# Block products in three wide projections of a two-block transformer kernel

## The chip, the cores and the metric

The kernel runs on one core of a Trainium2 chip. The metric is the time on the device from the start to the end of one execution, in microseconds. All data are fp32.

## What is computed

A first block (a Mamba-2 mixer with a mixture of experts, then differential attention with a mixture of experts) and a second block of two layers (three kinds of attention with a top-k choice of keys, then a gated MLP with a convolution). 256 tokens, width 1024. Cut to the three matrix products that the change touches, and to what is computed beside them:

```python
def diff_attention(x, cos, sin, w_qkv, ...):
    qkv = x @ w_qkv                      # 256x1024 @ 1024x3072
    q, k = apply_partial_rope(q), apply_partial_rope(k)
    ...                                  # 8 heads, two softmaxes each

# second block, each of two layers
z = rms_norm(h, g) @ w_in                # 256x1024 @ 1024x3016
c_q, c_kv, k_pe, dilated qkv, dsa qkv, q_idx, k_idx, w = split(z)
mla:     q = rms_norm(c_q) @ w_uq; kv = rms_norm(c_kv) @ w_ukv; rope
dilated: rope on q and k of 8 heads
dsa:     I[t, s] = sum_h w[t, h] * relu(q_idx[t, h] . k_idx[s])
         keep the 256 best causal keys of each row; rope
```

## The kernel before

The 256 tokens are two tiles of 128 (`tt` or `i` is 0 or 1). Weights come from memory as chunks of 1024 x 512 (2 MB) through `ring`, six slots that SyncE fills in order; a slot is released when the products that read it are done. All other data lie in one area of SBUF, `arena`. The five engines run their own lists of instructions, written out by hand, and wait for each other on semaphores; nothing reorders them.

**The projections.** `attention1` (`x @ w_qkv`) and `attention_layer(l)` for l = 0 and 1 (`h @ w_in`) each take six chunks. `PIECES` lists twelve pieces, a chunk `q` and a token tile. For each, `pe_project` makes eight matmuls of 128x512 (one for each 128 rows of the weights) into one of four PSUM banks, and ScalarE copies the bank to `qkv` or `zz` (`act_project`), in the second block with the row's 1/rms as the scale. The matmul is L1730, the copy L1739. One fp32 matmul stands as two passes in the trace.

**Beside them.** In attention1 VectorE makes the tables of sines, masks (`dve_dil_masks`, L1959 to L1962) and rotates q and k; TensorE then turns the heads (`pe_jobs`, L1759) once all twelve pieces are done, VectorE copies them (`dve_jobs`, L1769), and the attention units begin with L1831. GpSimd makes only `pool_affine` (L442, L443) there. In `attention_layer` VectorE rotates the index columns, normalises the latents (L2471 to L2480), multiplies the index scores by their weights after a relu (L2488), sums them (L2494), takes the best eight and strikes them out, eight times per tile (L2498, L2499), makes the mask, and rotates the MLA and dilated columns (L1799 to L1804). TensorE puts the turns, the index products (L2338) and the latent products (L2364, L2366) between pieces. GpSimd rotates the 512 DSA columns (L1785 to L1790) when all pieces are done.

**The MLP.** `mlp_layer` already makes its products from seven half-size ones. There VectorE forms the weight sums (L2719, L2723, L2725, 128x1024 each), GpSimd the token sums (L2694 to L2712, 128x256 and less), and the convolution's taps are added by VectorE from PSUM (L2737).

## Time and profile before

| | us |
|---|---|
| three runs | 2150.5, 2155.76, 2161.61 |
| median | 2155.76 |
| profiled execution | 2156.95 |
| its span, first to last instruction | 2154.9 |

The mean granted clock of TensorE over the span is 0.929. TensorE is busy for 86% of the span, VectorE for 36%, ScalarE for 18%, GpSimd for 7%.

The profile is read by stretch. The slices of the page show the DMA queues near 100% in the two mixtures of experts and below in the attention and MLP stages. The projections are then read by windows and by TensorE's timeline, and the cost of a new instruction by the groups that keep shapes apart. In the timeline a row is one or more equal instructions in succession; the bracket behind it is how long the engine had been idle, and what ended that.

### The profile page before, as it was taken

The numbers are of one execution on the slowest core, as the hardware profiler recorded it, in microseconds if no ns is written. First come the engines' busy times: TensorE is split into PE (matmuls) and PEld (weight loads), VectorE is DVE, ScalarE is ACT, GpSimd is POOL, SyncE is SP. The second block draws the span as 40 slices with busy tenths as digits, with TensorE's granted clock in tenths as the row PEclk, the third lists the DMA queues.
The fourth block names the chain that finished last, engine by engine and source line by source line (L and its number), as shares of the span: only waits on it lengthen the run. The fifth ranks groups of instructions, "written<-read, shape, count | busy, mean of one in ns | idle before, by whom it ended". The sixth has DMA issues, their size and how long they took to land.

```text
span 2154.9 us, 31628 instructions
## 1 busy us (share of the span) xinstructions
PE 1861.0 (86%) x12701; PEld 1144.9 (53%) x12701; DVE 776.9 (36%) x2404; ACT 380.7 (18%) x1032; POOL 153.5 (7%) x164
## 2 busy tenths in 40 slices
PE   8999999667666689898677676699999999999998
PEld 7687555333333344455333343345588744558873
DVE  4455343221222232653222222348333423833343
ACT  2122121111111111421110111113222101322110
POOL 0112100000000020000000000000002500000350
PEclk9999999988888999899887887899999999999999
DMA  9333379999999974279999999963154227324420
GB/s 353 119 118 117 120 288 424 423 423 422 425 425 423 413 261 156 76 317 422 426 422 423 425 423 423 391 230 117 53 178 147 113 93 267 117 72 163 156 98 30
DMA packets 116986, 565.23 MB, mean 262 GB/s; under 512 B 12968, under 2 KB 16238, under 8 KB 84078
## 3 DMA queue, kind: packets, MB, share of 16 engines
q1 hardware_dynamic: 116846, 563.21, 65.9%
q8 instruction: 107, 1.75, 0.3%
q14 instruction: 33, 0.27, 0.0%
HBM read 562.14 MB, written 1.05 MB: 261 GB/s over the span
## 4 chain that ended last, share of the span: by engine, by line
PE 62%; DMA 21%; SPq 10%; DVE 3%; ACT 2%; issue 2%; DVEq 0%; ACTq 0%
PE ps L2608 14%; DMA ring<-in_moe_w_down_dram 13%; PE ps L1730 12%; PE ps L2638 6%; SPq L844 6%; PE ps L1296 5%; PE ps L700 5%; DMA arena<-in_moe_w_up_dram 3%; PE ps L1402 3%; SPq L850 3%; PE ps L303 3%; PE ps L1306 3%; PE ps L740 2%; DMA arena<-in_moe_w_down_dram 2%; DMA ring<-in_moe_w_up_dram 2%
## 5 line engine op out<-in xcount | busy, mean ns | idle before, releaser
L2608 PE MATMUL ps<-arena,ring 128*128 128x256 f32 (+1 forms) x1536 | 305.5, 362 | 0.0
L2608 PEld LDWEIGHTS ps<-arena,ring 128*128 128x128 f32 x1536 | 271.9, 190 | 33.9 <-issue 1.0
L700 PE MATMUL ps<-ring,arena 128*32 128x256 f32 x2432 | 237.3, 434 | 50.6 <-issue 33.8
L1730 PE MATMUL ps<-ring,arena 128*128 128x512 f32 (+1 forms) x576 | 251.3, 595 | 3.6 <-DVE arena L428 3.6
L700 PE MATMUL ps<-arena 128*32 128x256 f32 x1536 | 179.3, 445 | 39.7 <-issue 29.8
L740 PE MATMUL ps<-ring,arena 128*32 128x256 f32 x1408 | 116.0, 485 | 80.6 <-DMA ring<-in_moe_w_down_dram 77.0
L1730 PEld LDWEIGHTS ps<-ring,arena 128*128 128x128 f32 x576 | 110.0, 193 | 136.3 <-issue 136.1
L700 PEld LDWEIGHTS ps<-ring,arena 128*32 128x32 f32 x2432 | 121.7, 124 | 109.0 <-issue 63.5
L716 DVE TENSOR_TENSOR arena<-arena,ps 64x256 f32<-64x256 f32 x64 | 27.2, 425 | 344.7 <-ACT arena L710 344.7
L2737 DVE SCALAR_TENSOR_TENSOR arena<-ps,pcol,arena 128x255 f32<-128x255 f32 (+1 forms) x176 | 84.9, 482 | 181.3 <-ACT arena L2676 178.2
L700 PEld LDWEIGHTS ps<-arena 128*32 128x32 f32 x1536 | 88.5, 127 | 99.8 <-issue 65.2
L759 DVE COPY h<-ps 32x256 f32<-32x256 f32 x128 | 54.3, 424 | 222.0 <-PE ps L740 221.1
L740 PEld LDWEIGHTS ps<-ring,arena 128*32 128x32 f32 x1408 | 53.4, 132 | 124.8 <-DMA ring<-in_moe_w_down_dram 83.0
L750 ACT ACTIVATE h<-ps 32x256 f32<-32x256 f32 x128 | 47.7, 373 | 396.7 <-PE ps L740 396.0
L1296 PE MATMUL ps<-arena,ring 128*128 128x256 f32 x512 | 116.4, 386 | 1.5 <-DMA ring<-in_ssm_w_in_dram 1.5
L1296 PEld LDWEIGHTS ps<-arena,ring 128*128 128x128 f32 x512 | 98.2, 194 | 15.3 <-issue 2.1
L740 PE MATMUL ps<-arena 128*32 128x256 f32 x640 | 54.9, 499 | 45.1 <-DMA arena<-in_moe_w_down_dram 42.6
L2676 ACT ACTIVATE arena<-ps,pcol 128x256 f32<-128x256 f32 x88 | 49.6, 563 | 232.9 <-PE ps L2608 232.7
L710 ACT ACTIVATE arena<-ps 64x256 f32<-64x256 f32 x64 | 24.0, 375 | 351.7 <-PE ps L700 351.7
L2707 POOL TENSOR_TENSOR arena<-arena 128x256 f32<-128x256 f32 x44 | 55.3, 1257 | 351.7 <-DVE arena L2737 351.7
L2638 PE MATMUL ps<-ring,arena 128*128 128x512 f32 x176 | 76.2, 592 | 0.0
L1574 DVE SCALAR_TENSOR_TENSOR arena<-ps,pcol,arena 128x255 f32<-128x255 f32 (+2 forms) x96 | 46.2, 481 | 62.0 <-ACT arena L1451 59.7
(339 smaller groups left out, 2210.2 us busy)
## 6 DMA issues: line engine op xcount, KB each, us to landing
ring<-in_moe_w_up_dram SPq DMA_DIRECT2D x44, 2048.0 KB, 36.9
ring<-in_moe_w_down_dram SPq DMA_DIRECT2D x44, 2048.0 KB, 35.4
ring<-in_moe_w_gate_dram SPq DMA_DIRECT2D x32, 2048.0 KB, 35.3
ring<-in_w_up_dram SPq DMA_DIRECT2D x22, 2048.0 KB, 8.0
arena<-in_moe_w_up_dram SPq DMA_DIRECT2D x20, 2048.0 KB, 37.2
arena<-in_moe_w_down_dram SPq DMA_DIRECT2D x20, 2048.0 KB, 36.2
...
```

Of the source, the lines that this page charges most:

```text
L303: return nc.tensor.matmul(ps[:, 4 + 2 * tt + half, :], lhs(4 * i + k, tt), w[:, k, half * 512:(half + 1) * 512], start=start, stop=stop)
L700: mm = nc.tensor.matmul(ps[j * CAP:(j + 1) * CAP, 5, 0:256], xg[:, b, (k % 2 * 4 + k // 2) * CAP:(k % 2 * 4 + k // 2 + 1) * CAP], w[k][:, ...
L740: mm = nc.tensor.matmul(ps[j * CAP:(j + 1) * CAP, 7, 0:256], hT[:, b, k % 2, (k // 2) * CAP:(k // 2 + 1) * CAP], wd[:, k, j * 256:(j + 1) ...
L844: sp.dma_start(dst, src[:, lo:hi, :]).then_inc(signal, 16)
L850: sp.dma_start(third_up if slot == 2 else ring.rows8(first + 3 * slot + 1), src).then_inc(signal, 16)
L1296: mm = nc.tensor.matmul(bank[:, 0:SEQ], w[:, k, k4 * P:(k4 + 1) * P], xT[:, k, :], start=(k == 0), stop=(k == KD - 1))
L1306: mm = nc.tensor.matmul(bank, xT[:, k, tt * P:(tt + 1) * P], w[:, k, :], start=(k == 0), stop=(k == KD - 1))
L1402: mm = nc.tensor.matmul(ps[:, part, :], yT[:, 4 * i + k, tt * P:(tt + 1) * P], w[:, k, half * 512:(half + 1) * 512], start=(i == 0 and k = ...
L1730: mm = nc.tensor.matmul(ps[:, bank + n % 4, 0:n_cols], xT[:, k, tt * P:(tt + 1) * P], w[:, k, :], start=(k == 0), stop=(k == KD - 1))
L2608: mm = nc.tensor.matmul(ps[:, n % 4, lo:hi], w[:, k, k4 * P:(k4 + 1) * P], xT_mlp[:, k, lo:hi], start=(k == 0), stop=(k == KD - 1))
L2638: mm = nc.tensor.matmul(ps[:, bank, :], lhs(i)[:, k, :], rhs(i)[:, k, :], start=(i == 0 and k == 0), stop=(i == 5))
L2737: ins = nc.vector.scalar_tensor_tensor(acc, ps[:, n % 4, 0:SEQ - 2 + j], taps2[j][:, n:n + 1], acc, ALU.mult, ALU.add)
```

## The change

Chunk 0 of each projection stays as it was. For chunks 1 to 5 the product of the 256x1024 tokens and the 1024x512 weights is split two by two: tokens into a(row, col), weights into b(row, col) of 512 x 256. Seven products of 128x512 by 512x256 (`BLOCKS`) take the place of eight. Each is four matmuls of 128x256 into one of banks 4 to 7 (`pe_block`, matmul L1804), and waits until the product four before it has been read.

- **Token sums.** VectorE forms S0 to S3 (128x512 each) once per projection.
- **Weight sums.** GpSimd forms T1 to T4 (128x1024 each, both inputs in SBUF) in each of the five chunks (`pool_weight_sum`, L1878, L1883, L1885, L1889). T1 of a chunk waits for P5 of the chunk before, T2 for its P6, T4 for P2 of its own chunk. P5, P6, P7 and P4 of a chunk read T1, T2, T3 and T4.
- **Results.** ScalarE copies P1 to two or three of the four output blocks (`act_first_block`); VectorE adds the other six into them from PSUM (`dve_block`, L1832 in attention1, L1833 with the row's 1/rms): 7 adds per chunk in attention1, 8 in the second block.
- **Ring.** The slots of chunks 1 to 5 are released at P4, the last product.
- **Moved or reshaped.** ScalarE takes the copies of the turned heads. In attention1 the turns are made after chunk 4 and inside chunk 5; `pool_affine` follows the 20 sums. In the second block ScalarE applies the relu to the index scores, and VectorE multiplies and sums them in eight instructions (`index_sums`, L2737 of the kernel after); the choice of the best keys is cut in parts that stand between the adds; the MLA and dilated rotation goes to GpSimd, after the sums of chunks 4 and 5.

```diff
+        BLOCKED = range(1, 6)
+        BLOCKS, BY_DVE = ("P1", "P2", "P6", "P7", "P5", "P3", "P4"), ("P2", "P6", "P7", "P5", "P3", "P4")
+        SUMS = ("T1", "T2", "T3", "T4")
...
+            n = product_count(name, c) - 1
+            if n >= 4:
+                freed, before = BLOCKS[(n - 4) % 7], (n - 4) // 7 + 1
+                if freed == "P1":
+                    pe.wait_ge(block_act.sem, block_act.at(before))
+                else:
+                    pe.wait_ge(block_dve.sem, block_dve.at(read_count(freed, before)))
...
+            elif name == "P6":
+                lhs, rhs = pj.S[1], pj.T2
+                pe.wait_ge(token_summed.sem, token_summed.at(2))
+                pe.wait_ge(weight_summed.sem, weight_summed.at(sum_count("T2", c)))
...
+            for k in range(4):
+                mm = nc.tensor.matmul(ps[:, bank_of(name, c), 0:256], lhs[:, k, :], rhs[:, k, :], start=(k == 0),
+                                      stop=(k == 3))
+            mm.then_inc(block_products.sem, 1)
...
+                (row, col), src = to, ps[:, bank_of(name, c), 0:256]
+                if pj.row_scale is None:
+                    return nc.vector.tensor_tensor(pj.out(c, *to), pj.out(c, *old), src, ALU.add)
+                return nc.vector.scalar_tensor_tensor(pj.out(c, *to), src, pj.row_scale[:, row:row + 1],
+                                                      pj.out(c, *old), ALU.mult, ALU.add)
...
+            if name == "T1":
+                ring.arrived(pool, pj.chunks[c])
+                if c >= 2:
+                    pool.wait_ge(block_products.sem, block_products.at(product_count("P5", c - 1)))
+                ins = nc.gpsimd.tensor_tensor(pj.T1, pj.b(c, 0, 1), pj.b(c, 0, 0), ALU.subtract)
+            elif name == "T2":
+                pool.wait_ge(weight_summed.sem, weight_summed.at(sum_count("T1", c)))
+                if c >= 2:
+                    pool.wait_ge(block_products.sem, block_products.at(product_count("P6", c - 1)))
+                ins = nc.gpsimd.tensor_tensor(pj.T2, pj.b(c, 1, 1), pj.T1, ALU.subtract)
+            elif name == "T3":
+                ins = nc.gpsimd.tensor_tensor(pj.b(c, 0, 1), pj.b(c, 1, 1), pj.b(c, 0, 1), ALU.subtract)
+            else:
+                pool.wait_ge(weight_summed.sem, weight_summed.at(sum_count("T2", c)))
+                pool.wait_ge(block_products.sem, block_products.at(product_count("P2", c)))
+                ins = nc.gpsimd.tensor_tensor(pj.b(c, 1, 0), pj.b(c, 1, 0), pj.T2, ALU.subtract)
+            ins.then_inc(weight_summed.sem, 1)
...
-            for q, c in enumerate(chunks):
-                ring.release(c, projected, PIECES.index((q, 1)) + 1)
-
-        def project_done(chunks):
-            projected.advance(2 * len(chunks))
-            projected_copied.advance(2 * len(chunks))
+            ring.release(chunks[0], projected, 2)
+            for c in BLOCKED:
+                ring.release(chunks[c], block_products, product_count("P4", c))
...
-            pe_project(pe, xT_first, c_qkv, 0, 1, 0, xT_ready)
+            pe_project(pe, pj1, 0, xT_ready)
             pe_turn_normed(pe, 1, -1)
-            pe_project(pe, xT_first, c_qkv, 1, 12, 0, xT_ready)
-            pe.wait_ge(projected_copied.sem, projected_copied.at(12))
-            pe.wait_ge(roped.sem, 1)
-            pe_jobs(pe, head_jobs)
+            for c in BLOCKED:
+                for name in BLOCKS:
+                    pe_block(pe, pj1, name, c)
+                    if (name, c) == ("P2", 1):
+                        pe_project(pe, pj1, 1, xT_ready)
+                    elif (name, c) == ("P4", 4):
+                        pe.wait_ge(roped.sem, 1)
+                        pe.wait_ge(projected_copied.sem, projected_copied.at(2))
+                        pe_jobs(pe, head_jobs[0:4])
+                    elif (name, c) == ("P6", 5):
+                        pe_jobs(pe, head_jobs[4:8], 4)
+            block_done(pe, 5)
...
+            for c in BLOCKED:
+                for name in SUMS:
+                    pool_weight_sum(pool, pj1, name, c)
...
+                if tt == 0:
+                    dve_block(dve, pj1, "P2", 4)
...
+                def index_sums(i):
                     kv = (i + 1) * P
-                    dve.wait_ge(idx_scores.sem, idx_scores.at(i + 1))
-                    for a in range(2):
-                        for m in range(4):
-                            ins = nc.vector.tensor_scalar(idx_terms[:, a, m, 0:kv], ps[:, m, a * SEQ:a * SEQ + kv],
-                                                          0.0, w_idx[:, i, 4 * a + m:4 * a + m + 1], ALU.max,
-                                                          ALU.mult)
-                    ins.then_inc(idx_read.sem, 1)
                     dve.wait_ge(idx_read.sem, idx_read.at(i + 1))
-                    wk = work[:, i, 0:kv]
-                    V(nc.vector.tensor_reduce(wk, idx_terms[:, :, :, 0:kv].rearrange("p a m k -> p k a m"),
-                                              XY, ALU.add))
-                    V(nc.vector.tensor_tensor(wk, wk, caus[i], ALU.add))
-                    for _ in range(TOPK // 8):
+                    for n in range(8):
+                        V(nc.vector.scalar_tensor_tensor(work[:, i, 0:kv], idx_terms[:, n // 4, n % 4, 0:kv],
+                                                         w_idx[:, i, n:n + 1], work[:, i, 0:kv] if n else caus[i],
+                                                         ALU.mult, ALU.add))
...
+                dve_block(dve, pj, "P2", 2)
+                dve_block(dve, pj, "P6", 2)
+                dve_block(dve, pj, "P7", 2)
+                index_sums(0)
+                dve_block(dve, pj, "P5", 2)
+                dve_block(dve, pj, "P3", 2)
+                take_best(0, 0, 2)
+                dve_block(dve, pj, "P4", 2)
+                take_best(0, 2, 6)
+                dve_block(dve, pj, "P2", 3)
...
+                dve_block(dve, pj, "P2", 4)
+                mask_others(1)
+                dve.wait_ge(lat_copied.sem, lat_copied.at(1))
+                lat_heads(0)
+                dve_block(dve, pj, "P6", 4)
+                dve_block(dve, pj, "P7", 4)
+                lat_heads(1)
```

In GpSimd's list, first layer of the second block, this stood before: the affine step of the block before, then the rotation of the DSA columns.

```order
47 L442 TENSOR_TENSOR h<-arena 128x8x128
48 L443 TENSOR_TENSOR h<-h,arena 128x8x128
49 L442 TENSOR_TENSOR h<-arena 128x8x128
50 L443 TENSOR_TENSOR h<-h,arena 128x8x128
51 L1785 TENSOR_TENSOR arena<-arena,cst 128x64
52 L1786 TENSOR_TENSOR arena<-arena,cst 128x64
53 L1787 TENSOR_TENSOR arena<-arena,cst 128x64
54 L1788 TENSOR_TENSOR arena<-arena,cst 128x64
```

After the change, from the same place (T1, T2, T3, T4 of chunks 1 and 2; `piece_ready` counts the block products there, `z_tanh_done` the weight sums):

```order
71 L1878 TENSOR_TENSOR arena<-ring 128x1024 [waits slot1_loaded,moe_down]
72 L1883 TENSOR_TENSOR arena<-ring,arena 128x1024 [waits z_tanh_done,h_ready]
73 L1885 TENSOR_TENSOR ring<-ring 128x4x256
74 L1889 TENSOR_TENSOR ring<-ring,arena 128x4x256 [waits piece_ready,z_tanh_done]
75 L1878 TENSOR_TENSOR arena<-ring 128x1024 [waits piece_ready,slot2_loaded]
76 L1883 TENSOR_TENSOR arena<-ring,arena 128x1024 [waits piece_ready,z_tanh_done]
77 L1885 TENSOR_TENSOR ring<-ring 128x4x256
78 L1889 TENSOR_TENSOR ring<-ring,arena 128x4x256 [waits piece_ready,z_tanh_done]
```

Eight of twenty weight sums are shown; the rotation of the DSA columns comes after all of them.

In VectorE's list, first layer of the second block, the sums and the choice for the first token tile stood in one piece (L2488 to L2499), behind the copies of turned data:

```order
1013 L1769 COPY arena<-ps 128x512
1014 L1769 COPY arena<-ps 128x256
1015 L2488 TENSOR_SCALAR arena<-ps,tiny 128x128 x8
1016 L2494 TENSOR_REDUCE arena<-arena 128x128
1017 L2496 TENSOR_TENSOR arena<-arena,cst 128x128
1018 L2498 MAX arena<-arena 128x8
1019 L2499 MATCH_REPLACE arena<-arena 128x128
1020 L2498 MAX arena<-arena 128x8
```

After the change the adds of block products (L1833) stand ahead of the index sums (L2737), and between the parts of the choice (L2744, L2745):

```order
1025 L2731 MEMSET tiny 128x6
1026 L1833 SCALAR_TENSOR_TENSOR arena<-ps,tiny,arena 128x256 x4
1027 L2737 SCALAR_TENSOR_TENSOR arena<-arena,tiny,cst 128x128
1028 L2737 SCALAR_TENSOR_TENSOR arena<-arena,tiny 128x128 x7
1029 L1833 SCALAR_TENSOR_TENSOR arena<-ps,tiny,arena 128x256 x3
1030 L2744 MAX arena<-arena 128x8
1031 L2745 MATCH_REPLACE arena<-arena 128x128
1032 L2744 MAX arena<-arena 128x8
1033 L2745 MATCH_REPLACE arena<-arena 128x128
1034 L1833 SCALAR_TENSOR_TENSOR arena<-ps,tiny,arena 128x256
```

Four adds moved ahead of the sums; P5 and P3 of chunk 2 are read only behind the eight sums.

In TensorE's list, attention1, the turns of heads (L1759) stood behind all pieces:

```order
474 L412 MATMUL ps<-cst,arena 128x128 x8
475 L1730 MATMUL ps<-ring,arena 128x512 x8
476 L412 MATMUL ps<-cst,arena 128x128 x8
477 L1730 MATMUL ps<-ring,arena 128x512 x88
478 L1759 MATMUL ps<-cst,arena 128x128 x32
479 L1831 MATMUL ps<-arena 128x128 x2
```

After the change the last part of it, chunks 4 and 5 with the turns (L1912) in two groups:

```order
491 L1804 MATMUL ps<-arena 128x256 x4
492 L1804 MATMUL ps<-ring,arena 128x256 x4
493 L1804 MATMUL ps<-arena 128x256 x4
494 L1804 MATMUL ps<-ring,arena 128x256 x8
495 L1912 MATMUL ps<-cst,arena 128x128 x16
496 L1804 MATMUL ps<-ring,arena 128x256 x8
497 L1804 MATMUL ps<-arena 128x256 x4
498 L1912 MATMUL ps<-cst,arena 128x128 x16
499 L1804 MATMUL ps<-ring,arena 128x256 x4
500 L1804 MATMUL ps<-arena 128x256 x4
501 L1804 MATMUL ps<-ring,arena 128x256 x8
502 L1993 MATMUL ps<-arena 128x128 x2
```

Sixteen turns moved ahead of chunk 5, sixteen behind its third and fourth product.

## Rows read from the trace of the kernel before

**Rows 1.** Which stretch: three projections; us, busy by engine (count), clock, DMA share, GB/s

```profile
764.00:850.00 86.00, 85.96 (x200) 38.14 (x200) 15.51 (x49) 10.77 (x20) 9.57 (x3) 0.97 0.54 196
...
1400.00:1480.00 80.00, 80.00 (x235) 37.70 (x234) 46.30 (x156) 14.81 (x32) 0.00 (x0) 1.00 0.58 210
1780.00:1860.00 80.00, 80.00 (x244) 38.24 (x243) 45.96 (x170) 11.03 (x23) 0.00 (x0) 1.00 0.60 222
```

**Rows 2.** Groups by form, TensorE: busy us, mean ns of one

```profile
L2608 PE MATMUL ps<-arena,ring 128*128 128x256 f32 x1280 | 276.6, 379 | 0.0
...
L1730 PE MATMUL ps<-ring,arena 128*128 128x512 f32 x512 | 225.3, 598 | 2.0 <-DVE arena L428 2.0
```

**Rows 3.** Timeline of TensorE, attention1: start us, us, what xcount [idle before]

```profile
764.00 9.55 PE L1730 MATMUL ps<-ring,arena 128*128 128x512 f32 x16 [2.02 <-DVE arena L428]
...
774.26 75.70 PE L1730 MATMUL ps<-ring,arena 128*128 128x512 f32 x176
850.65 3.89 PE L1759 MATMUL ps<-cst,arena 128*128 128x128 f32 x32 [0.69 <-ACT arena L1739]
856.28 0.93 PE L1831 MATMUL ps<-arena 64*128 64x128 f32 x8 [1.74 <-DVE arena L1769]
```

**Rows 4.** Timeline of TensorE, second layer of the second block

```profile
1780.56 33.75 PE L1730 MATMUL ps<-ring,arena 128*128 128x512 f32 x80
...
1830.14 1.15 PE L2338 MATMUL ps<-arena 32*128 32x256 f32 x16
...
1866.81 1.36 PE L1831 MATMUL ps<-arena 96*128 96x128 f32 x7
```

**Rows 5.** Groups by form, GpSimd

```profile
L1533 POOL TENSOR_TENSOR arena<-arena 128x512 f32<-128x512 f32 x16 | 16.6, 1040 | 50.4 <-ACT arena L1479 50.4
...
L2694 POOL TENSOR_TENSOR arena<-arena 128x256 f32<-128x256 f32 x10 | 7.2, 724 | 0.8
...
L442 POOL TENSOR_TENSOR h<-arena 128x1024 f32<-128x1024 f32 x2 | 5.7, 2868 | 508.6 <-ACT arena L398 508.6
L1541 POOL TENSOR_TENSOR arena<-arena 128x256 f32<-128x256 f32 x8 | 5.1, 635 | 19.0 <-DVE arena L1636 19.0
...
L1785 POOL TENSOR_TENSOR arena<-arena,cst 128x64 f32<-128x64 f32 x4 | 1.3, 327 | 863.4 <-ACT arena L1739 863.4
```

**Rows 6.** Timeline of both engines, 1708 to 1713 us

```profile
1708.33 1.57 POOL L2707 TENSOR_TENSOR arena<-arena 128x256 f32<-128x256 f32 x1 [1.88 <-DVE arena L2737]
...
1709.23 1.75 DVE L2725 TENSOR_TENSOR ring<-ring 128x1024 f32<-128x1024 f32 x1
...
1709.98 1.31 POOL L2694 TENSOR_TENSOR arena<-arena 128x128 f32<-128x128 f32 x1
```

**Rows 7.** Groups by form, VectorE

```profile
L2737 DVE SCALAR_TENSOR_TENSOR arena<-ps,pcol,arena 128x255 f32<-128x255 f32 x88 | 42.5, 483 | 178.2 <-ACT arena L2676 178.2
...
L2719 DVE TENSOR_TENSOR arena<-ring 128x1024 f32<-128x1024 f32 x10 | 12.1, 1215 | 0.0
...
L1932 DVE SCALAR_TENSOR_TENSOR arena<-arena,tiny 128x256 f32<-128x256 f32 x8 | 3.9, 484 | 0.3
...
L1932 DVE SCALAR_TENSOR_TENSOR arena<-arena,tiny 128x128 f32<-128x128 f32 x8 | 2.8, 351 | 0.3
...
L1799 DVE TENSOR_TENSOR arena<-arena,cst 128x36 f32<-128x36 f32 x4 | 0.8, 198 | 14.0 <-ACT arena L1739 14.0
```

**Rows 8.** Timeline of both engines, 763 to 768 us

```profile
763.05 3.80 POOL L443 TENSOR_TENSOR h<-h,arena 128x1024 f32<-128x1024 f32 x1
...
764.88 1.99 DVE L262 SCALAR_TENSOR_TENSOR tiny<-tiny 128x1 f32<-128x1 f32 x1
...
767.21 0.16 DVE L262 SCALAR_TENSOR_TENSOR tiny<-tiny 128x1 f32<-128x1 f32 x1
```

**Rows 9.** Windows around the start of attention1's projection

```profile
760.00:764.00 4.00, 1.95 (x8) 1.60 (x9) 2.59 (x7) 1.50 (x4) 3.83 (x2) 0.50 1.03 362
...
768.00:772.00 4.00, 4.00 (x9) 1.67 (x8) 1.22 (x2) 1.23 (x1) 2.53 (x1) 0.88 1.03 387
```

More of the change, by code:

```diff
@@ L1117, in experts_dve @@
                 normalise(1)
+                if layer == 1:
+                    dve.wait_ge(rows_loaded.sem, 64)
+                    dve_second_rows(dve, 0)
                 affine(1)
@@ L1772, in dve_jobs, with act_jobs @@
                 ins.then_inc(jobs_copied.sem, 1)
+        def act_jobs(act, jobs, first=0):
+            for m, (blocks, dst, gain) in enumerate(jobs, first):
+                act.wait_ge(jobs_turned.sem, jobs_turned.at(m + 1))
+                src = ps[0:blocks[0].shape[1], m % 4, 0:len(blocks) * P]
+                if len(dst.shape) == 3:
+                    src = src.rearrange("p (a b) -> p a b", a=dst.shape[1])
+                nc.scalar.activation(dst, src, ACT.Copy, scale=1.0 if gain is None else gain)\
+                    .then_inc(jobs_copied.sem, 1)
         def jobs_done(n):
@@ L2469, in dve_attention @@
                 V(nc.vector.tensor_scalar(w_idx, zz[:, :, Z_W:N_IN2], 256 ** -0.5, None, ALU.mult))
+                nc.vector.memset(rms_t, 0.0).then_inc(ready2.sem, 1)
+                for name in BY_DVE[1:]:
+                    dve_block(dve, pj, name, 1)
                 dve.wait_ge(lat_squared.sem, lat_squared.at(1))
@@ new lines, in dve_attention @@
+                mask_others(1)
[4 more added lines that the diff above has]
+                lat_heads(1)
+                dve_block(dve, pj, "P5", 4)
+                dve_block(dve, pj, "P3", 4)
+                nc.vector.memset(rms_t, 0.0).then_inc(ready2.sem, 1)
+                dve_block(dve, pj, "P4", 4)
+                for name in BY_DVE:
+                    dve_block(dve, pj, name, 5)
```

363 lines of the change are left out of this document (263 added, 100 removed).

## Prediction

> **What bounds the kernel now.** I read the windows of the three projections first [rows 1]. TensorE is busy for 85.96 of 86 us in attention1 and for all 80.00 us in each layer of the second block, at a granted clock of 0.97 to 1.00 of full speed. VectorE is busy for 15.5 us there in attention1 and for 46 us in the second block, GpSimd for 9.6 us and nothing. The DMA share is 0.54 to 0.60, so the weights come ahead of use. The projections are bound by TensorE alone: 1 us of matmul removed is 1 us gained, for as long as TensorE never waits. The timelines of TensorE show no idle time between the pieces [rows 3, 4]. The stage behind attention1 streams the experts' weights and starts when the ring's slots come free, so a shift of an attention stage passes on to the end one to one.
>
> **What the change removes.** A pass of 128x512 takes 0.429 us: 80 passes in 33.75 us with the neighbours' overlap give 0.42 to 0.43 [rows 4], 176 in 75.70 give 0.430 [rows 3], and the group gives 225.3/512 = 0.44 with the slow-clock ones in it. A pass of 128x256 takes 276.6/1280 = 0.216 us [rows 2]. A chunk was 16 matmuls of two passes, 32 x 0.429 = 13.7 us; it becomes 28 of two passes, 56 x 0.216 = 12.1 us. The gain is 1.63 us a chunk, 8.15 a projection, 24.4 us in all. In attention1 half of the turns (3.89 us) with the idle 0.69 and 1.74 us around them [rows 3] come inside the projection, where copies lie beside products: another 2.4 us.
>
> **What GpSimd gets.** 20 sums of 128x1024 per projection. No row has this form with both inputs contiguous in SBUF. From 64 to 256 elements a sum goes from 327 to 724 ns, 2.07 ns an element [rows 5]; continued to 1024 that is 0.72 + 768 x 0.00207 = 2.3 us. Lower end: from 256 to 512 elements it goes from 635 to 1040 ns, 1.58 ns an element, which gives 1.85 us. Upper end: L442, 128x1024 with one strided side, 2.87 us [rows 5]. I take 2.3, since it comes from the same kind of sums (L2694) as the new ones. Four sums are 9.2 us of a chunk's 12.1 us. T1 to T3 start together when P5 of the chunk before ends and run for 6.9 us; P6 comes 6.9 us and P7 8.7 us behind that P5, and T2 is ready after 4.6, T3 after 6.9 us. Undisturbed, GpSimd keeps up with 1.8 to 2.3 us to spare.
>
> **What it does to VectorE.** This is the term that decides. In the MLP both engines do weight and token sums side by side [rows 6]: GpSimd's L2707 runs from 1708.33 to 1709.90; VectorE's L2725, begun at 1709.23, ends 1.08 us behind that end; and GpSimd's next, begun at 1709.98, ends only behind L2725. They take 1.57 and 1.75 us, where the same forms alone take 0.72 [rows 5] and 1.22 us [rows 7]. At 764.88 it is plainer [rows 8]: a VectorE instruction on a single column, 0.16 us alone, takes 1.99 us, because L443 of GpSimd, begun at 763.05, ends at 766.85. So a VectorE instruction with two inputs from SBUF stands still until the sum that runs on GpSimd is over, and they take turns, one for one. L2737, with PSUM as one of its inputs, has a mean of 483 ns [rows 7] and shows nothing of the kind beside GpSimd's token sums; the 115 new adds are of its form, 0.48 us each, and I charge them no waits.
>
> The Trainium skill says this in "SBUF — State Buffer", section "Who interferes with whom": a VectorE instruction with two SBUF inputs contends with a GpSimd instruction that reads SBUF, and whoever holds the shared port pair blocks the other fully; with at most one SBUF input and no two-port mode there is no contention. By that rule the trace agrees (1.99 us for 0.16). It speaks against this change, for a burst of T1 to T3 can hold up three VectorE instructions for a sum each. If one took rows 6 to be a slowdown by some tenths only, the sum below would end below the time before.
>
> What has two SBUF inputs on VectorE in the second block: the rotations (six instructions each, 0.2 us and up [rows 7]), the index sums, eight of 0.35 us for tile 0 and eight of 0.48 for tile 1 [rows 7], the masks, the token sums, parts of each 1/rms. In all VectorE has about 56 us of own work in 85 us of projection; adds are 40 x 0.48 = 19 us of it. Each stretch of such work that meets a burst is longer by up to 6.9 us, and the adds queued behind it on VectorE come later. Product n waits until product n-4 was read, so TensorE stops.
>
> **The walk**, with those durations in the order of the new lists; "stall" is TensorE idle.
> - attention1. The lambda and mask instructions (from 789.6 before) stand ahead of P6's add in chunk 1 and meet T1 to T3 of chunk 2: P6 is read at 798.6, P4 waits, stall 7.1 us. The rotation of q and k, 12 large instructions, stands in chunk 4 and meets T3, T4 and the next T1 to T3: stall 7.5 us, in front of the first turns. Stalls 14.6, gains 8.15 + 2.4 and a little cover: +4.4 us.
> - second block, layer 0. 1/rms comes late, stall 2.6; the index rotation in chunk 1 meets T1 to T3 of chunk 2, and `ready2` comes 6.9 us later: stall 9.0. Then as layer 1. In sum +20.8 us.
> - layer 1. The first part is just in time (0.6 us to spare). `index_sums(0)`, 3.1 us of work, meets T1 to T3 of chunk 3 and lasts from 1810.7 to 1819.1: stall 4.4. `index_sums(1)` meets the burst of chunk 4, from 1829.3 to 1838.9: stall 2.5, and 2.4 more at the choice. `mask_others(1)` and `lat_heads(0)` meet that of chunk 5: stall 7.3. 16.6 of stalls and 0.7 of ends, less 8.15: the units start at 1876.0 in place of 1866.81 [rows 4], +9.2 us.
>
> Sum: 4.4 + 20.8 + 9.2 = +34.4 us.
>
> **The clock.** Around attention1's start TensorE was busy for 1.95 of 4 us and the granted clock is 0.50 [rows 9]; the first 16 passes took 9.55 in place of 6.9 us [rows 3]. So a long stop can cost another 2.7 us afterwards. There are five stalls of 7 us or more: 0 to 13 us, I take 3. On the other side the units of attention1 begin with TensorE warmer: 0 to 2 us back. Net +1.
>
> Profiled execution 2156.95 + 34.4 + 1 = 2192; the median of the runs is 1.2 us below the profiled one, so 2190 us. With sums of 1.85 us a burst is 5.6 us and the same walk gives about +28 less 6 where rotations slip between bursts: 2178. Should every other stall be half hidden, 2165. With the clock's upper end 2203.
>
> **What a rule would have instead.** The Trainium skill, "GPSIMD Engine Reference", section 4.1, gives an elementwise sum of two inputs to VectorE, as about twice as fast. On this kernel's rows, VectorE's 128x1024 takes 1.22 us [rows 7] against my 2.3: 20 sums would be 24 us on an engine with 56 of work in 85, and nothing would contend. By that rule the change put the sums on the wrong engine. That is also an experiment.
>
> **Rivals.**
> - *The queues keep up* (other side). The bursts fall between VectorE's two-input stretches, or the adds' slack of four products (6.9 us) absorbs a burst. Then the gain stands: 2156.95 - 24.4 - 2.4 - 2 = 2129, range 2124 to 2145. For it: the slack is as long as a burst, and VectorE is busy for 66% only. Against: two-input work is placed directly in front of adds, in each of the chunks 1 to 5. It decides from the point at which all stalls together stay below 16 us.
> - *The gain is eaten up.* Half of the collisions happen, stalls of 27 us in place of 60: 2157, within 0.5%.
> - *GpSimd becomes the bound.* Sums at L442's 2.87 us: 11.5 of 12.1 us a chunk, T3 is ready 8.6 us behind P5 with 0.05 to spare, and every turn that VectorE takes, and the rotations now in its list (12 and more instructions after chunk 4), delay a product of TensorE directly. 2 to 4 us a chunk over 15 chunks less what is counted above: 2205 to 2215.
>
> **How the numbers follow.** Forecast (stalls exceed the gain, 2165 to 2205) 0.47, GpSimd the bound 0.12, gain eaten up 0.16, queues keep up 0.25. Slower by over 0.5% (10.8 us, about what a measurement can tell from no change) is 0.47 + 0.12 = 0.59; within it 0.16; faster 0.25. Both signs hold much, so the range has to reach from the rival's 2130 to 2210; the likeliest one's own range is 2165 to 2205.
>
> **What would show it.** Right: in the new trace VectorE's L2737 (`index_sums`) has a mean of over 0.8 us in place of 0.35 to 0.48, single ones 2 us and more; TensorE's timeline has idle times of 4 to 9 us behind `<-DVE` at P4 of chunks 1 and 4 and at P2 of chunk 3; L1878 to L1889 take 2.3 us alone; the adds stay at 0.48 us. The units of layer 0 start about 21 us later in their stage, those of layer 1 about 9. Wrong: TensorE's busy share stays at 1.00 from chunk 1 to 5; or its waits name GpSimd, which is the third rival; or sums of under 1.5 us. The walk is weakest in layer 0, where several short works stand close together, and where 5 us either way hang on the order in which two engines reach the same point.

## The result

| | us |
|---|---|
| before, median of four runs beside the change | 2156.07 (2150.5 to 2161.61) |
| after, median of four runs | 2191.85 (2185.03 to 2196.41) |
| ratio after to before | 1.0164, interval 1.0149 to 1.0179 |
| span of the profiled execution after | 2190.4, granted clock 0.921 |

The change makes the kernel slower by 1.6%. The forecast was 2190 us. Below, a stop is a time in which TensorE stands idle.

### The profile page after: what moved, and what is told of

It is laid out like the page before. It is cut to its first block, busy times and chain, and to the rows that moved or that the text cites. A ratio compares the mean times of both kernels' runs of the same rounds, so it can differ in the third digit from the quotient of the medians.

```text
span 2190.4 us, 32731 instructions
## 1 busy us (share of the span) xinstructions
PE 1850.2 (84%) x13061; PEld 1221.1 (56%) x13061; DVE 866.8 (40%) x2435; ACT 399.1 (18%) x1088; POOL 315.7 (14%) x276
## 4 chain that ended last, share of the span: by engine, by line
PE 55%; DMA 20%; SPq 10%; DVE 9%; ACT 2%; issue 2%; DVEq 0%; ACTq 0%
PE ps L2875 14%; DMA ring<-in_moe_w_down_dram 13%; PE ps L2905 6%; SPq L848 6%; PE ps L704 5%; PE ps L1303 5%; PE ps L1804 5%; DMA arena<-in_moe_w_up_dram 3%; PE ps L303 3%; PE ps L744 3%; PE ps L1409 3%; PE ps L1313 3%; SPq L854 2%; DMA arena<-in_moe_w_down_dram 2%; DMA ring<-in_moe_w_up_dram 2%
## 5 line engine op out<-in xcount | busy, mean ns | idle before, releaser
L2875 PEld LDWEIGHTS ps<-arena,ring 128*128 128x128 f32 x1536 | 271.9, 190 | 33.9 <-issue 1.0
L704 PE MATMUL ps<-arena 128*32 128x256 f32 x1536 | 170.3, 431 | 39.4 <-issue 27.5
L1878 POOL TENSOR_TENSOR arena<-ring 128x1024 f32<-128x1024 f32 x15 | 35.7, 2382 | 1150.6 <-DMA ring<-in_w_in_dram 595.8
L1804 PE MATMUL ps<-ring,arena 128*128 128x256 f32 x600 | 149.5, 402 | 40.6 <-DVE arena L1833 26.9
L720 DVE TENSOR_TENSOR arena<-arena,ps 64x256 f32<-64x256 f32 x64 | 27.2, 425 | 352.6 <-ACT arena L714 352.5
L3004 DVE SCALAR_TENSOR_TENSOR arena<-ps,pcol,arena 128x255 f32<-128x255 f32 (+1 forms) x176 | 84.8, 482 | 181.4 <-ACT arena L2943 178.2
L1804 PEld LDWEIGHTS ps<-ring,arena 128*128 128x128 f32 x600 | 118.7, 202 | 63.5 <-DVE arena L1833 30.4
L744 PE MATMUL ps<-arena 128*32 128x256 f32 x640 | 58.0, 523 | 43.8 <-DMA arena<-in_moe_w_down_dram 41.5
```

Source lines behind the costliest of these rows:

```text
L704: mm = nc.tensor.matmul(ps[j * CAP:(j + 1) * CAP, 5, 0:256], xg[:, b, (k % 2 * 4 + k // 2) * CAP:(k % 2 * 4 + k // 2 + 1) * CAP], w[k][:, ...
L744: mm = nc.tensor.matmul(ps[j * CAP:(j + 1) * CAP, 7, 0:256], hT[:, b, k % 2, (k // 2) * CAP:(k // 2 + 1) * CAP], wd[:, k, j * 256:(j + 1) ...
L1804: mm = nc.tensor.matmul(ps[:, bank_of(name, c), 0:256], lhs[:, k, :], rhs[:, k, :], start=(k == 0), stop=(k == 3))
L2875: mm = nc.tensor.matmul(ps[:, n % 4, lo:hi], w[:, k, k4 * P:(k4 + 1) * P], xT_mlp[:, k, lo:hi], start=(k == 0), stop=(k == KD - 1))
L3004: ins = nc.vector.scalar_tensor_tensor(acc, ps[:, n % 4, 0:SEQ - 2 + j], taps2[j][:, n:n + 1], acc, ALU.mult, ALU.add)
```

## The profile after

The same three stretches as [rows 1], moved with the start of each projection (columns: us, busy time of PE, PEld, DVE, ACT, POOL with counts, granted clock, DMA share, GB/s):

```profile
764.00:850.00 86.00, 72.33 (x285) 55.92 (x286) 48.57 (x81) 10.43 (x23) 43.58 (x18) 0.89 0.48 175
1407.30:1487.30 80.00, 70.87 (x302) 53.42 (x300) 67.82 (x156) 19.32 (x47) 40.76 (x28) 0.93 0.50 182
1805.40:1885.40 80.00, 66.36 (x301) 51.80 (x300) 70.92 (x163) 14.65 (x37) 47.37 (x31) 0.94 0.53 196
```

TensorE, busy for all of every stretch before, is busy for 72.33 of 86, 70.87 of 80 and 66.36 of 80 us. VectorE's time rose from 15.5 to 48.6 and from 46 to 68 and 71 us; the new adds are 15 and 19 us of it. GpSimd is busy for half of each stretch, as worked out. The shares of the DMA engines did not rise.

TensorE's timeline of attention1 answers [rows 3]; the second fence, of the second block's layer 1, answers [rows 4]:

```profile
763.87 8.49 PE L1770 MATMUL ps<-ring,arena 128*128 128x512 f32 x16 [2.02 <-DVE arena L428]
...
797.15 7.23 PE L1804 MATMUL ps<-ring,arena 128*128 128x256 f32 x24 [6.69 <-DVE arena L1832]
...
842.47 3.78 PE L1804 MATMUL ps<-ring,arena 128*128 128x256 f32 x8 [6.99 <-DVE arena L1832]
846.04 3.16 PE L1912 MATMUL ps<-cst,arena 128*128 128x128 f32 x16
...
863.55 0.93 PE L1993 MATMUL ps<-arena 64*128 64x128 f32 x8 [0.51 <-DVE arena L1832]
```

```profile
1798.99 6.28 PE L1770 MATMUL ps<-ring,arena 128*128 128x456 f32 x16
...
1845.23 3.68 PE L1804 MATMUL ps<-ring,arena 128*128 128x256 f32 x8 [3.80 <-DVE arena L1833]
...
1865.15 1.99 PE L1804 MATMUL ps<-ring,arena 128*128 128x256 f32 x8 [0.93 <-DVE arena L1833]
...
1874.39 1.99 PE L1804 MATMUL ps<-ring,arena 128*128 128x256 f32 x8 [2.07 <-DVE arena L1833]
1883.03 7.02 PE L1804 MATMUL ps<-ring,arena 128*128 128x256 f32 x24 [6.64 <-DVE arena L1833]
...
1902.23 1.99 PE L1993 MATMUL ps<-arena 96*128 96x128 f32 x12
```

Each stop shown ends with an add of a block product (L1832, L1833) on VectorE. Layer 0 has stops of 2.71, 3.88, 0.92, 2.07 and 6.64 us; the first of them ends with a copy of ScalarE, the others with such adds. All stops of the three projections together are 44.1 us. From the projection's start to the first attention unit it is 99.68 us in attention1 (92.28 before), 111.21 in layer 0 (94.74) and 103.24 in layer 1 (93.25). The starts of the three projections stand 640.96 and 394.16 us apart (633.53 and 376.03 before) and from the last start to the end of the span it is 391.4 us (381.3 before). So attention1 cost 7.4, layer 0 18.1 and layer 1 10.1 us: 35.6 us, the whole difference of the spans (35.5). Of this 33.9 us lie ahead of the first attention units, and 1.7 us behind the first unit of layer 0.

What VectorE did in the first stop, with GpSimd beside it (both engines, start, us):

```profile
788.88 2.51 POOL L1878 TENSOR_TENSOR arena<-ring 128x1024 f32<-128x1024 f32 x1 [9.19 <-PE ps L1804]
789.23 2.58 DVE L2122 SCALAR_TENSOR_TENSOR cst<-cst,arena 128x384 f32<-128x384 f32 x1
791.47 2.53 POOL L1883 TENSOR_TENSOR arena<-ring,arena 128x1024 f32<-128x1024 f32 x1
791.84 2.31 DVE L2123 TENSOR_TENSOR cst<-cst 128x128 f32<-128x128 f32 x1
793.97 2.38 POOL L1885 TENSOR_TENSOR ring<-ring 128x1024 f32<-128x1024 f32 x1
794.19 2.45 DVE L2124 TENSOR_TENSOR cst<-cst 128x256 f32<-128x256 f32 x1
796.67 1.92 DVE L1832 TENSOR_TENSOR arena<-arena,ps 128x256 f32<-128x256 f32 x4
```

Three mask instructions with two inputs in SBUF, which took 0.56, 0.29 and 0.43 us before, take 2.58, 2.31 and 2.45 us, one for each sum T1, T2, T3. P6's add, the first of the four in the last row, is behind them. That is the mechanism of [rows 8], now three times in a row. The groups by form of GpSimd and VectorE say the same in the mean:

```profile
L1883 POOL TENSOR_TENSOR arena<-ring,arena 128x1024 f32<-128x1024 f32 x15 | 36.0, 2400 | 11.8 <-DVE h L632 10.7
L1878 POOL TENSOR_TENSOR arena<-ring 128x1024 f32<-128x1024 f32 x15 | 35.7, 2382 | 1150.6 <-DMA ring<-in_w_in_dram 595.8 <-DMA ring<-in_attn_w_qkv_dram 508.8 <-PE ps L1804 45.9
```

```profile
L1833 DVE SCALAR_TENSOR_TENSOR arena<-ps,tiny,arena 128x256 f32<-128x256 f32 x80 | 36.7, 481 | 34.0 <-PE ps L1804 30.2 <-ACT arena L1818 1.5
...
L2737 DVE SCALAR_TENSOR_TENSOR arena<-arena,tiny 128x256 f32<-128x256 f32 x14 | 18.6, 1328 | 0.5
...
L1832 DVE TENSOR_TENSOR arena<-arena,ps 128x256 f32<-128x256 f32 x35 | 14.7, 420 | 36.6 <-PE ps L1804 35.7
...
L2737 DVE SCALAR_TENSOR_TENSOR arena<-arena,tiny 128x128 f32<-128x128 f32 x14 | 12.9, 924 | 0.5
```

A sum takes 2.38 to 2.49 us (the forecast's 2.3). The index sums take 0.92 and 1.33 us on the mean in place of the 0.35 and 0.48 of the same form in [rows 7]. The adds from PSUM take 0.48 and 0.42 us, where the forecast charged 0.48 for all; those that ran beside a weight sum took the same.

## The experiments

Each was timed beside the kernel before on the same chip, and ratios are to that kernel. It took 2157.43 us beside the first four experiments and 2154.07 us beside the last three, and each ratio is known to about 0.2% (4 us), so small differences between two experiments are read from the traces and not from the times. Code is cut to the lines that matter.

### Without the weight sums

```diff
-                lhs, rhs = pj.S[0], pj.T1
+                lhs, rhs = pj.S[0], pj.b(c, 0, 0)
...
-            for c in BLOCKED:
-                for name in SUMS:
-                    pool_weight_sum(pool, pj1, name, c)
```

> The changed kernel with all 60 weight sums on GpSimd left out (P5 and P6 read blocks of the weights as they are, P7 and P4 read unsummed ones); everything else in place and in order. Theory (each VectorE instruction with two SBUF inputs waits for a whole sum on GpSimd): TensorE's idle times of 3.8 to 7.0 us in the projections vanish, TensorE waits for under 8 us in all three together instead of 43.5, and with the stops the half-speed stretches behind them go; time 2128 us (2120 to 2140), VectorE's index sums (L2737) at 0.35 and 0.48 us. Rival (the adds of block products merely stand behind too much work in VectorE's list, whatever GpSimd does): at least 25 us of waiting stay, time 2160 to 2180.

TensorE's waits for the weight sums go with them. The products are made of unsummed weights, so this run measures time and gives no usable projection.

Measured: 2127.65 us, ratio 0.9854 (0.9837 to 0.9871), as expected. A stretch of 80 us of layer 0, from 5.8 us behind the start of its projection (2.5 in the stretch of the change):

```profile
1390.10:1470.10 80.00, 80.00 (x390) 64.71 (x389) 54.14 (x177) 22.31 (x55) 8.33 (x26) 1.00 0.55 203
```

TensorE is busy for 80.00 of 80 us, and there is no stop over 0.3 us in the three projections but one of 0.51 us ahead of attention1's first unit. Projection to first unit takes 82.4, 87.9 and 84.8 us where before it was 92.3, 94.7 and 93.3. The index sums are back at 0.35 and 0.49 us. The order of VectorE's list is untouched, so the rival that blames the order alone falls. This run takes away TensorE's own waits for GpSimd as well; but no stop of the changed kernel names GpSimd, and the next runs keep those waits. It also measures what the block products are worth when nothing stands in their way: 28.4 us of span, against the 24.4 + 2.4 + up to 2 of the forecast.

### The same sums in four pieces each

```diff
+            def parts(out, x, y):
+                for k in range(0, 4, 1):
+                    ins = nc.gpsimd.tensor_tensor(out[:, k:k + 1], x[:, k:k + 1], y[:, k:k + 1], ALU.subtract)
+                return ins
...
-                ins = nc.gpsimd.tensor_tensor(pj.T1, pj.b(c, 0, 1), pj.b(c, 0, 0), ALU.subtract)
+                ins = parts(pj.T1, pj.b(c, 0, 1), pj.b(c, 0, 0))
```

> Each weight sum on GpSimd is made as four instructions of 128x256 in place of one of 128x1024. Theory (turns are taken instruction by instruction): a two-input instruction of VectorE waits 0.7 us at most in place of 2.4, so stretches of few instructions get shorter (attention1's masks: stall 6.7 to about 2.5; rotation of q and k: 7.0 to about 4), the eight index sums gain nothing (eight turns cost 8 x 0.72), and GpSimd's own work rises from 9.6 to 11.6 of 12.1 us a chunk; time 2180 us (2170 to 2190). Rival (the two engines share a resource in proportion, or GpSimd's total work is what matters): the longer bursts make every stall longer, 2200 us or more.

Measured: 2164.1 us, ratio 1.0035 (1.0018 to 1.0052), below the range expected. GpSimd and VectorE at the index sums of tile 0, layer 1:

```profile
1812.10 2.83 POOL L1876 TENSOR_TENSOR arena<-ring 128x256 f32<-128x256 f32 x4 [2.41 <-PE ps L1804]
...
1814.38 5.17 DVE L2742 SCALAR_TENSOR_TENSOR arena<-arena,tiny 128x128 f32<-128x128 f32 x7
1815.00 2.93 POOL L1876 TENSOR_TENSOR arena<-ring,arena 128x256 f32<-128x256 f32 x4
...
1817.89 2.92 POOL L1876 TENSOR_TENSOR ring<-ring 128x256 f32<-128x256 f32 x4
...
1820.51 1.78 PE L1804 MATMUL ps<-ring,arena 128*128 128x256 f32 x7 [1.41 <-DVE arena L1833]
```

Seven index sums take 5.17 us (6.68 beside whole sums), about one piece of 0.72 us each. Total work on GpSimd grew (11.7 us a chunk, 9.7 with whole sums), yet the kernel is 28 us faster than with whole sums. So what counts is how long one instruction on GpSimd is, and how many of VectorE's meet it. The theory's sign is right and the rival is out. The size was 28 us in place of my 12. The masks' stop fell from 6.69 to 2.47 us as expected; that at the rotation of q and k fell from 6.99 us to nothing (I expected 4), and those behind the first index sums from 3.88 and 3.80 to 0.74 and 1.41 us (I expected no gain). All stops fell from 44.1 to 27.2 us; slow passes behind them, which I had not counted, went with some. In the profiled execution 5.6 us of the difference stand ahead of attention1's projection, where the two kernels are equal; whether the other runs have that too is not known. One stop of the third rival's kind appeared, 1.12 us with GpSimd as the releaser in attention1. And layer 0 stopped for 6.06 us at its first turns, which the next runs explain.

### TensorE kept busy in four of the stops

```diff
                 for name in BLOCKS:
+                    if (name, c) in (("P4", 1), ("P4", 4)):
+                        pe_stay_awake(pe, 2, 7)
                     pe_block(pe, pj1, name, c)
...
+                        if (name, c) == ("P4", 4):
+                            pe.wait_ge(lat_copied.sem, lat_copied.at(1))
+                            pe_stay_awake(pe, 2, 7)
                         pe_block(pe, pj, name, c)
```

> The changed kernel with seven matmuls of 128x512 (6.0 us) that no one reads, put in front of P4 of chunks 1 and 4 in attention1 and of chunk 4 in each layer of the second block, where TensorE stands still for 6.6 to 7.0 us. Theory (a stop costs again in granted clock afterwards): the slow passes behind these four stops go (1.9 + 3.1 + 2.1 + 1.7 us), time 2183 us (2180 to 2187). Rival (the clock falls for another reason, or the stops hide it): 2190 to 2194.

Measured: 2186.93 us, ratio 1.0138 (1.0116 to 1.0159): some 5 us less than the change alone, but the intervals of the two ratios overlap, so the time alone does not decide. The windows of both around the stop in chunk 4 of attention1, first of the change, then of this kernel:

```profile
840.00:844.00 4.00, 1.53 (x4) 1.26 (x5) 3.60 (x7) 0.00 (x0) 1.26 (x1) 0.50 0.00 0
844.00:848.00 4.00, 4.00 (x16) 3.42 (x15) 0.84 (x2) 0.61 (x2) 0.00 (x0) 0.50 0.20 29
```

```profile
840.00:844.00 4.00, 3.00 (x13) 1.92 (x12) 3.53 (x8) 0.00 (x0) 0.77 (x1) 1.00 0.00 0
844.00:848.00 4.00, 4.00 (x28) 3.72 (x27) 0.42 (x1) 2.58 (x6) 0.00 (x0) 1.00 0.66 242
```

After 6.99 us without work TensorE has a granted clock of 0.50 (1.2 GHz) for more than 4 us; kept busy, 1.00 (2.4 GHz). P4's eight passes take 3.78 us in the one and 1.99 in the other. From start to first unit attention1 takes 95.24 in place of 99.68 us, the layers 109.81 for 111.21 and 101.26 for 103.24, 7.8 us in all of the 8.8 expected, although the first passes of attention1 and layer 0 were 1.3 and 0.4 us slower in this execution. Of attention1's 4.4 us only 1.7 are left at the start of the next projection, and the median shows 4.9 in all. That the slow passes come from the stops is shown by the granted clock and the times of the passes (3.78 and 1.99 us); the saving in the total is likely and not more.

### The sums on VectorE

```diff
+        def dve_piece(dve, pj, name, c):
+            dve_block(dve, pj, name, c)
+            if name == "P2":
+                dve_weight_sum(dve, pj, "T4", c)
+            elif name in ("P5", "P3", "P4") and c < 5:
+                dve_weight_sum(dve, pj, {"P5": "T1", "P3": "T2", "P4": "T3"}[name], c + 1)
```

> All weight sums are made by VectorE between its adds (T4 behind P2, T1, T2, T3 of the next chunk behind P5, P3, P4); GpSimd keeps its rotations and the affine step. Theory (the exclusive use of the SBUF port pair is the cost): no VectorE instruction of these stretches takes over 1.3 us; in attention1 VectorE has room (about 55 of 82 us), so the stage gains its 8 to 12 us; in the second block it has about 81 us of work for 77 us of TensorE's, so 5 to 12 us of waiting stay in each layer and the gain is about used up; time 2148 us (2138 to 2165). Rival (VectorE lacks throughput, GpSimd's port does not matter): 24 us more work per projection on the busy engine, time 2200 us or more.

Measured: 2145.08 us, ratio 0.9935 (0.9918 to 0.9952), as expected. It is 47 us less than the change (49 by the ratios), with 24 us more of work per projection on the busier engine: 60 sums of 1.22 us. Attention1 takes 82.74 us (82.39 without any sums), layer 0 95.72 and layer 1 91.81, with stops of 7.1 and 4.8 us left in the layers. The rival (VectorE lacks throughput, 2200 us or more) is out; whether the stops left in the layers are lack of time or order of work is tested by the last run. This is also the experiment that the forecast named where it set VectorE against GpSimd for these sums: here the slower engine was not too slow, it was in the way.

### The affine step first, and an odd mask

```diff
+            pool.wait_ge(rows_loaded.sem, 32)
+            pool_affine(pool)
             for c in BLOCKED:
                 for name in SUMS:
                     pool_weight_sum(pool, pj1, name, c)
-            pool.wait_ge(rows_loaded.sem, 32)
-            pool_affine(pool)
...
-                    V(nc.vector.tensor_scalar(wk, wk, TAKEN, NEG, ALU.not_equal, ALU.mult))
+                    nc.vector.tensor_scalar(wk[:, 0:kv - 1], wk[:, 0:kv - 1], TAKEN, NEG, ALU.not_equal, ALU.mult)
```

> The changed kernel with two small edits in different stages. In attention1 GpSimd's affine step (L442, L443) stands again ahead of the 20 weight sums: the first attention unit waited 4.17 us for VectorE, whose L2092 took 3.00 us beside L443. Theory: that wait falls to about 1.4 us as in the kernel before, and the weight sums of chunk 1, now starting near 775 us, are still ready for P6 at 783: time 2188 us (2185 to 2191). Rival (the wait belongs to the unit itself): no change, 2191 to 2195. In the second block the mask's TENSOR_SCALAR, which took 2.18 us beside a weight sum with only one SBUF input, is made on an odd number of columns (127 or 255, and one more instruction for the last column). If the even count let it into a two-port form, it now takes under 0.6 us, and the next instruction waits in its place, so that no time is won; if any VectorE instruction is stopped by GpSimd, it stays at 2 us.

Measured: 2194.61 us, ratio 1.0193 (1.0169 to 1.0216). No gain: it is above the range expected, and the ratio's interval overlaps the change's. The first unit's wait fell from 4.17 to 1.45 us as expected, but attention1's stage (640.46 us to the next projection's start, 640.96 in the change) is as long as it was: the sums of chunk 1 now met three of the four token sums, which took 2.7 to 2.8 us for 0.69, and the first unit started 100.64 us behind the projection's start in place of 99.68. Moving GpSimd's work moves the collision.

The mask on 255 columns:

```profile
L2751 DVE TENSOR_SCALAR arena<-arena 128x255 f32<-128x255 f32 x2 | 4.3, 2166 | 0.0
```

It still takes 2.17 us (0.29 us for 256 columns in the kernel before, where GpSimd did nothing beside it), so an even count of columns is not what exposes it. The Trainium skill, "VectorE: DVE Perf Modes", section "Mode 2×_2P — use both read ports for one tensor", lets an odd count in as well where source and destination have the same; by that rule the trace agrees, and my alternative of an odd mask could not have helped.

The unexpected part is layer 0, whose instructions up to that point are the same as in the change. TensorE waits for the index rotation, L1961 to L1966 on 36 columns:

```profile
1426.50 1.99 PE L1804 MATMUL ps<-arena 128*128 128x256 f32 x8 [2.72 <-ACT arena L1818]
...
1428.64 2.34 POOL L1878 TENSOR_TENSOR arena<-ring 128x1024 f32<-128x1024 f32 x1 [5.76 <-PE ps L1804]
1428.69 2.34 DVE L1961 TENSOR_TENSOR arena<-arena,cst 128x36 f32<-128x36 f32 x1
...
1431.06 2.39 POOL L1883 TENSOR_TENSOR arena<-ring,arena 128x1024 f32<-128x1024 f32 x1
...
1431.17 2.33 DVE L1964 TENSOR_TENSOR arena<-arena,cst 128x36 f32<-128x36 f32 x1
1433.41 2.33 POOL L1885 TENSOR_TENSOR ring<-ring 128x1024 f32<-128x1024 f32 x1
1433.53 2.26 DVE L1965 TENSOR_TENSOR arena<-arena 128x36 f32<-128x36 f32 x1
...
1436.65 1.51 PE L1912 MATMUL ps<-cst,arena 128*128 128x128 f32 x6 [8.16 <-DVE tiny L2719]
```

Three rotation instructions of 0.2 us are stopped by T1, T2 and T3, and TensorE stands for 8.16 us. In the profiled execution of the change the same rotation ended at 1433.14 and its T1 began at 1433.48: it slipped through by 0.3 us. The traces show why. T1 waits for the end of P5 of the chunk before, and P5 follows a stop of 2.7 us:

```profile
1429.56 3.78 PE L1804 MATMUL ps<-arena 128*128 128x256 f32 x8 [2.71 <-ACT arena L1818]
```

This is P5 in the change, 3.78 us at a granted clock of 0.50 (1.2 GHz); the first row above is the same P5 in this run, 1.99 us at 1.00 (2.4 GHz). The rotation starts 1.04 us behind P5's start in both, T1 3.92 us behind it in the one and 2.14 in the other. The five traces with sums on GpSimd all fit: where P5 was slow (the change, 3.78 us; the filled stops, 3.50) the rotation slipped through, and where it took 1.99 us (here, the sums in pieces, the index scores from PSUM) TensorE stopped for 8.16, 6.06 and 8.16 us. So the slow clock saved a stop, and luck decided. It also shows that one and the same stop of 2.7 us is followed by slow passes in some executions and not in others; why is not shown.

Layer 0 takes 117.9 us here and 111.2 there. Whether this divides the change's runs (2185 to 2196 us) is not shown: only one of them has a trace, and the kernel before spreads as widely (2150.5 to 2161.6).

### The index scores from PSUM

```diff
+                            ins = nc.vector.tensor_scalar(idx_terms[:, a, m, 0:kv], ps[:, m, a * SEQ:a * SEQ + kv],
+                                                          0.0, w_idx[:, i, 4 * a + m:4 * a + m + 1], ALU.max,
+                                                          ALU.mult)
...
-                        V(nc.vector.scalar_tensor_tensor(work[:, i, 0:kv], idx_terms[:, n // 4, n % 4, 0:kv],
-                                                         w_idx[:, i, n:n + 1], work[:, i, 0:kv] if n else caus[i],
-                                                         ALU.mult, ALU.add))
+                    wk = work[:, i, 0:kv]
+                    V(nc.vector.tensor_reduce(wk, idx_terms[:, :, :, 0:kv].rearrange("p a m k -> p k a m"),
+                                              XY, ALU.add))
```

ScalarE's relu of the scores is left out, since the multiplies now do it.

> The changed kernel, but VectorE makes relu and weight of the index scores from PSUM (8 instructions per tile) and one reduction, as in the kernel before, in place of eight sums with two SBUF inputs. Own work of VectorE rises from 3.1 to 5.0 us for tile 0 and from 3.9 to 7.8 us for tile 1. Theory (two SBUF inputs beside GpSimd are the cost): the sums no longer wait for T1 to T3, TensorE's stops at P2 of chunk 3 (3.9 us) and P2 of chunk 4 (0.9 us) go to under 1.5 us together in each layer, with 2 us of slow clock; time 2184 us (2179 to 2189), though VectorE does more. Rival (the length of VectorE's list is the cost): 5.8 us more of work per layer make the stops longer, time 2195 to 2203.

Measured: 2177.35 us, ratio 1.0104 (1.0087 to 1.0121), some 14 us less than the change (13 by the ratios) although VectorE works more, and a little below the range expected. Both engines at tile 0, layer 1:

```profile
1833.36 2.35 POOL L1878 TENSOR_TENSOR arena<-ring 128x1024 f32<-128x1024 f32 x1 [2.83 <-PE ps L1804]
1834.07 2.15 DVE L2728 TENSOR_SCALAR arena<-ps,tiny 128x128 f32<-128x128 f32 x8
1835.80 2.36 POOL L1883 TENSOR_TENSOR arena<-ring,arena 128x1024 f32<-128x1024 f32 x1
1836.25 1.96 DVE L2737 TENSOR_REDUCE arena<-arena 128x128 f32<-128x1024 f32 x1
...
1838.11 2.35 POOL L1885 TENSOR_TENSOR ring<-ring 128x1024 f32<-128x1024 f32 x1
1838.24 2.37 DVE L2739 TENSOR_TENSOR arena<-arena,cst 128x128 f32<-128x128 f32 x1
...
1850.38 1.54 PE L1912 MATMUL ps<-cst,arena 128*128 128x128 f32 x6 [5.08 <-DVE arena L2728]
```

Eight multiplies from PSUM take 2.15 us and the reduction 1.96 us, both unhindered beside T1 and T2; the single addition with two SBUF inputs (0.29 us alone) takes 2.37. The stop at P2 of chunk 3 went from 3.80 to 0.51 us, as the theory has it, and the rival (a longer list makes longer stops) is out. But the rest of the 14 us is not a proof of the theory. A new stop of 1.32 us came at the index products, and one of 5.08 us at the latent turns, which now wait for VectorE's multiplies of tile 1; my expectation had not priced them. And the stops of 2.07 and 6.64 us in chunk 4 are gone, though the edit does not touch what stands there: the mask on 256 columns (0.90 us) and its addition (0.43 us) now end before T1 of chunk 5 begins. Layer 1 is 6.4 us shorter, and that is more than the index sums gave. Moving the work moved the collisions again, this time to the good. The profiled execution has the 8.16 us stop of layer 0, so the median is the better figure here.

### The sums on VectorE, the late choice spread

```diff
+                take_best(1, 1, 2)
+                dve_piece(dve, pj, "P4", 4)
+                take_best(1, 2, 4)
+                dve_piece(dve, pj, "P2", 5)
+                take_best(1, 4, 6)
+                dve_piece(dve, pj, "P6", 5)
...
+                dve_piece(dve, pj, "P5", 5)
+                mask_others(1)
```

The parts of tile 0's choice are also set a little later in chunk 3.

> All weight sums on VectorE (as in the run with the sums on VectorE), and the choice of the best keys of tile 1 and its mask, which no one reads before the tenth attention unit, spread over chunks 4 and 5, where VectorE had 1 to 5 us of idle time. Theory: TensorE's stops in layer 0 (7.0 us, of them 3.1 at P4 of chunk 4's neighbour and 1.7 at the start) and layer 1 (5.8 us) fall to 3 us and 1 us, with 1 us of slow clock each; time 2137 us (2132 to 2142), faster than both kernels. Rival (VectorE is short of time through the whole projection): 2143 to 2148.

Measured: 2135.6 us, ratio 0.9917 (0.9902 to 0.9933), faster than both kernels and as expected. Three stretches of the same lengths, from 0.04, 0.05 and 6.49 us behind the starts of the projections:

```profile
763.60:849.60 86.00, 83.19 (x365) 65.18 (x365) 57.42 (x123) 14.79 (x37) 9.66 (x3) 0.97 0.57 206
1386.50:1466.50 80.00, 77.29 (x346) 59.27 (x347) 71.87 (x184) 20.61 (x50) 9.98 (x26) 0.98 0.60 218
1766.20:1846.20 80.00, 78.86 (x392) 64.70 (x390) 74.40 (x193) 20.72 (x49) 9.96 (x26) 1.00 0.60 221
```

TensorE is busy for 77.3 to 79 of 80 us in the layers with VectorE at 72 and 74 us, more than in the change. Stops are 2.7 and 1.1 us, in place of 7.1 and 4.8. So VectorE was not short of time in the layers; its work stood in the wrong places, and the rival is out by the traces. By the ratios alone this run and the one before it with sums on VectorE (0.9917 and 0.9935) are not told apart. From the run without any sums it is 8 us away by the medians and 14 by the ratios.

## Why the prediction held, step by step

- *TensorE alone is the bound, as long as it never waits.* Right. Without the sums 25.2 us went out of the three projections and 28.4 out of the span.
- *The removed passes.* Eight passes of 128x256 take 1.73 us from start to start in the new timeline, the forecast's 0.216 us each.
- *GpSimd's sums, 2.3 us.* 2.38 to 2.49 us. The stretch from 64 and 256 elements to 1024 held. GpSimd was not the bound; the third rival showed in one stop of 1.1 us, with pieces.
- *A VectorE instruction with two SBUF inputs waits for a whole sum.* Right, shown three ways: the sums left out, cut, and moved. It is not only those with two inputs (see the end).
- *Adds from PSUM are free of it.* Right (0.42 and 0.48 us).
- *Attention1.* Stops: forecast 7.1 and 7.5, measured 6.69 and 6.99, at the products named. Stage +4.4 forecast, +7.4 measured, since the slow passes were missing. Behind the first unit a wait grew from 1.38 to 4.17 us, because L2092 took 3.00 us beside GpSimd's affine step (L443), which the change had moved there; but TensorE's granted clock over the first 19.5 us of the units was 0.82 in place of 0.74, and the rest of the stage is as long as before (541.3 us).
- *Layer 1.* Forecast 4.4, 2.5, 2.4 and 7.3; measured 3.80, 0.93, 2.07 and 6.64. Stage +9.2 forecast, +10.1 measured.
- *Layer 0.* Forecast +20.8, with a stop of 9.0 at the index rotation; measured +18.1 without it. The stop is real (8.16 us in two other runs with the same instructions there), but it hangs on how fast P5 ran. That the sum still came near is luck.
- *The clock.* The mis-sized term. I took the time from projection start to first unit, left out the stops and the passes up to P1 of chunk 1 (whose clock differs from execution to execution), and set it against the run without sums: it is longer by 5.0 us in attention1, 8.4 in layer 0 and 4.8 in layer 1. That is 18 us where I took 3 with an upper end of 13. I had counted stops of 7 us or more; stops of 2.7 and 3.9 us also left slow passes behind. This is a difference of two kernels and not all of it need be clock; the run with filled stops shows 7.8 us of it for four stops.

So the stops were over-sized (about 60 us forecast, 44.1 measured) and the clock under-sized (3 for about 18), and the two errors cancel to within 2 us. The total agreed better than its terms deserve. The sum has two slips of about 1 us as well: 2156.95 + 34.4 + 1 less 1.2 is 2191, and the first rival's sum is 2128.

Rivals: *the queues keep up* fails on the point it named, stops below 16 us; they were 44. *The gain is eaten up* would have needed 27. *GpSimd becomes the bound* would show waits for GpSimd, and no stop of the changed kernel names it.

## What to carry to other kernels

Work given to an idle GpSimd is free only where VectorE has nothing with two inputs in SBUF to do at that moment; read VectorE's list beside it, and where both must run, keep GpSimd's instructions short or take one of VectorE's inputs from PSUM. When TensorE is the bound, a stop costs its length and, often, slow passes after it (here about 18 us behind 44 us of stops). And an engine busy for 90% can be the right place for more work if its instructions are hardly ever stopped. Where two engines meet by chance, as at the index rotation, one profiled execution does not tell what the others do.

## What had not been expected

- A TENSOR_SCALAR with one SBUF input is stopped too: the mask on 128x256 took 2.18 us for 0.29, a TENSOR_SCALAR on two columns 2.32 for 0.16, and an odd count of columns did not spare it. "SBUF — State Buffer", section "Who interferes with whom", of the Trainium skill names this form among those that can take the shared pair; the trace agrees, and I had left it out of the walk. TENSOR_SCALARs on a single column were not stopped beside L443 or a weight sum (0.15 and 0.27 us); L262 of [rows 8] has one column too, but two SBUF inputs, and was. Maximum (0.43 us on 256 columns), match-and-replace (0.41), the reduction (1.96) and the adds from PSUM (0.42 and 0.48) ran at their own time beside a weight sum.
- The turns are not strictly one for one. In layer 0 of the run with the affine step first, two instructions of 36 columns (L1962, L1963) passed between T1 and T2. So what a stretch loses is set by the sums that it meets, at most one stopped instruction for each in these traces.
